# Encoder layer with experts: x tiles turned inside spans of 256 tokens, the first expert's row list by one-hot products, the last output tile in another order, the value slices asked for sooner

## The reference, cut to what matters

```python
def encoder(x, ...):                                  # x_prompt: 256 tokens, x_sample: 1024 tokens, D = 1024
    xn = rmsnorm(x, norm1_g)
    proj = xn @ w_in                                  # columns: pool u (512), q, k, v, o (512 each), 16 gates
    a = multiscale_pool(proj[u], pool_w, pool_scale)
    m = bidir_mlstm(proj, gate_b, head_norm_g)        # 4 heads of 128, chunks of 128 tokens, two directions
    x = x + concat(a, m) @ w_out
    xn2 = rmsnorm(x, norm2_g)
    x = x + hier_moe(xn2, ...)                        # best of 4 groups, best 2 of its 8 experts, SwiGLU
    return rmsnorm(x, final_norm_g)

def hier_moe(xn, ...):
    # each token chooses 2 of 32 experts; rows are sorted by expert, in blocks of 128
    hb = silu(xb @ w_gate[e]) * (xb @ w_up[e])        # 1024 x 512 each
    y  = hb @ w_down[e]                               # 512 x 1024
    return segment_sum(y[dest] * weight, token)
```

## Time and profile before

| what | us |
|---|---|
| median of 3 runs | 1238.58 (1236.71 to 1238.65) |
| the profiled execution, its own time | 1236.62 |
| its span, first to last instruction | 1234.9 |
| TensorE matmul busy | 1113.7 (90%) |
| VectorE busy | 866.8 (70%) |
| ScalarE busy | 684.6 (55%) |
| mean granted TensorE clock | 0.962 |

### The profile page before, as it was taken

The page is one execution under the profiler, slowest core; times in us unless marked ns, Lnnn a source line. Parts: engine busy times, 40 slices in busy tenths (PEclk is TensorE's granted clock), DMA queues, the critical chain, the costliest instruction groups (busy, mean ns, idle before and its releaser), DMA issues.

```text
span 1234.9 us, 17854 instructions
## 1 busy us (share of the span) xinstructions
PE 1113.7 (90%) x5679; PEld 935.0 (76%) x5679; DVE 866.8 (70%) x1340; ACT 684.6 (55%) x1128; POOL 185.3 (15%) x285
## 2 busy tenths in 40 slices
PE   5999999998998999992899999999999999999910
PEld 4888888887888788881688888888888888888710
DVE  5649510234447656665688999999999999999958
ACT  5432241233346544213677877877787787787623
POOL 1100210011100012223011211221221221121100
PEclk9999999999999899995899999999999999999965
DMA  8212240455979344446789999999999999999667
GB/s 236 59 29 83 86 129 1 142 175 199 318 265 334 130 139 151 163 154 228 269 313 374 372 377 385 378 380 391 382 380 394 382 378 391 383 372 387 241 251 298
DMA packets 135808, 324.04 MB, mean 262 GB/s; under 512 B 23552, under 2 KB 60320, under 8 KB 135760
## 3 DMA queue, kind: packets, MB, share of 16 engines
q1 hardware_dynamic: 119856, 281.80, 63.1%
q0 software_dynamic: 15904, 41.61, 8.7%
HBM read 285.35 MB, written 51.11 MB: 272 GB/s over the span
## 4 chain that ended last, share of the span: by engine, by line
PE 78%; DVE 9%; ACT 6%; DMA 3%; issue 3%; POOL 0%; ACTq 0%; SPq 0%; POOLq 0%; DVEq 0%
PE psum L808 23%; PE psum L810 22%; PE psum L809 22%; DVE e_lo L1723 3%; ACT e_hi L1284 3%; PE psum L1024 2%; PE psum L979 1%; PE psum L1057 1%; ACT h_fb L1241 1%; DVE x L1834 1%; DVE x L1842 1%; PE psum L922 1%; DVE x L1832 1%; PE psum L863 1%; PE psum L967 1%
## 5 line engine op out<-in xcount | busy, mean ns | idle before, releaser
L1723 DVE TENSOR_TENSOR e_lo<-e_st,e_hi 128x1024 fp32r<-128x1024 f32 x384 | 442.6, 1219 | 15.6 <-ACT e_hi L1284 14.4
L1284 ACT ACTIVATE e_hi<-e_st 128x1024 fp32r<-128x1024 f32 x384 | 372.3, 1053 | 9.4 <-PE psum L810 8.4
L808 PE MATMUL psum<-e_hi,ex_hi 128*128 128x512 f32 x512 | 203.8, 398 | 8.6 <-DVE ex_lo L1765 3.7
L810 PE MATMUL psum<-e_hi,ex_lo 128*128 128x512 f32 x512 | 200.8, 392 | 0.0
L809 PE MATMUL psum<-e_lo,ex_hi 128*128 128x512 f32 x512 | 200.3, 391 | 0.0
L808 PE MATMUL psum<-xT_hi,w_hi 128*128 128x512 f32 (+1 forms) x408 | 147.1, 361 | 4.5 <-DVE xT_lo L1403 3.0
L809 PE MATMUL psum<-xT_lo,w_hi 128*128 128x512 f32 (+1 forms) x408 | 145.4, 356 | 0.0
L810 PE MATMUL psum<-xT_hi,w_lo 128*128 128x512 f32 (+1 forms) x408 | 145.3, 356 | 0.0
L808 PEld LDWEIGHTS psum<-e_hi,ex_hi 128*128 128x128 f32 x512 | 96.6, 189 | 41.4 <-DVE e_lo L1723 16.3
L810 PEld LDWEIGHTS psum<-e_hi,ex_lo 128*128 128x128 f32 x512 | 96.5, 189 | 20.8
L809 PEld LDWEIGHTS psum<-e_lo,ex_hi 128*128 128x128 f32 x512 | 96.6, 189 | 19.3
(11 more groups left out here) (234 smaller groups left out, 1722.3 us busy)
## 6 DMA issues: line engine op xcount, KB each, us to landing
e_st<-in_expert_w_gate_dram SPq DMA_DIRECT2D x128, 512.0 KB, 4.7
e_st<-in_expert_w_up_dram SPq DMA_DIRECT2D x128, 512.0 KB, 7.3
e_st<-in_expert_w_down_dram SPq DMA_DIRECT2D x128, 512.0 KB, 8.6
mlstm_units<-stage SPq DMA_DIRECT2D x18, 640.0 KB, 3.8
w_st<-in_w_in_dram SPq DMA_DIRECT2D x20, 512.0 KB, 4.1
xn_scratch<-xn POOLq DMA_DIRECT2D x20, 512.0 KB
f_y<-expert_rows SPq DMA_DIRECT2D x20, 512.0 KB, 12.1
stage<-gate_rows SPq DMA_DIRECT2D x18, 512.0 KB, 6.0
```

The costliest lines, as they stand in the source:

```text
L808: pe.matmul(out, a_hi, b_hi, start=start, stop=False)
L810: return pe.matmul(out, a_lo, b_hi, start=False, stop=stop)
L1284: act.activation(e_hi[:, r, :, :], e_st[:, slot, :, :], ACT.Copy).then_inc(ehi_done, 1)
L1723: dve.tensor_tensor(e_lo[:, r, :, :], e_st[:, slot, :, :], e_hi[:, r, :, :].bitcast(F32), ALU.subtract).then_inc(elo_done, 1)
```

## The change

1. Start. The first six products are the three pool slices over tokens 0 to 255 and then over 256 to 511 (`SPANS`), in place of three over 0 to 511. Only tiles 0 and 1 are turned before them; tiles 2 and 3 inside products 0 and 1, the others behind products 2 to 6. Small products on the identity (`keep_warm`) stand between. ScalarE and VectorE run roots, norms and splits in a written order (`x_root`, `x_norm`). Slices 1 and 2 and x tile 2 are asked for when tile 1 has landed; the gate slice comes before the other constants; the gate bias has a semaphore of its own.
2. SyncE asks for slices 19 and 20 at block 6 of its loop, ahead of that block's store.
3. Output stage. The heads of tile 2 are turned after tile 0's products and its squares are taken later. For the last tile, ranks and turns of the tiles before it are put between halves of its products, the turned last tile is copied before its squares are taken, and filler products (`keep_busy`, 128 x 512 into a free bank) stand around the router.
4. First list. `list_rows` also compares the slot number of expert 0 with a ramp, which gives a one-hot matrix of token by slot for each tile. Ten products with `token_parts` (token in tile, tile, second choice, one) give, per slot, the row number; three VectorE operations make `first_row` of it, and the first gather uses it. The last list entries are written after that gather is issued; the other lists go the old way.
5. `gx` is set to zero when the turn of the output loop on GpSimd reaches tile 8. The last router's weights are worked out later. Four pieces of expert 1 are asked for when the first gather has landed, ahead of the load of the lists.
6. Expert rows are turned and split in two halves with a signal each, in all steps.

```diff
-        proj += [("u", U + c, 0) for c in range(NG - 1)]
+        proj += [("u", U + c, NS + half) for half in range(2) for c in range(NG - 1)]
...
             slice_in(0)
+            sp.wait_ge(x_load[1], 16)
             slice_in(1)
+            slice_in(2)
+            sp.wait_ge(bias_zero, 1)
...
+            slice_in(G)
...
-                if i == N_EARLY - 1:
+                if i == N_EARLY - 2:
                     for m in (NSL - 2, NSL - 1):
                         slice_in(m)
                 block_out(i)
...
+            sp.wait_ge(gx_load[0], 16)
+            for c in range(4):
+                gu_in(1, c)
             for i in range(2):
                 sp.wait_ge(list_out[i], 16 * NT)
...
             for i, t in enumerate(order):
+                if i == NT - 2:
+                    pool.wait_ge(hT_ready, NT)
+                    pool.memset(gx[:, :, :], 0.0).then_inc(gx_zero, 1)
+                if i == NT - 1:
+                    entries_out(i - 1)
                 pool.wait_ge(xn2_done, i + 1)
...
             pool.wait_ge(gx_zero, 1)
+            pool.wait_ge(totals_read, 1)
+            rows_in(0, 0)
+            entries_out(NT - 1)
             pool.wait_ge(first_rows, 16)
-            rows_in(0, 0)
             rows_in(1, 1)
...
+            keep_warm(8)
+            x_transposes(0)
+            keep_warm(3)
+            x_transposes(1)
+            keep_warm(8)
+            transposed_inside = {0: 2, 1: 3}
+            transposed_after = {2: (4,), 3: (5,), 4: (6,), 5: (7,), 6: (8, 9)}
...
+            out_rows(NT - 1, 0, 0, 4)
+            ranks(NT - 3)
+            x1_transposes(NT - 2)
+            out_rows(NT - 1, 0, 4, KD)
+            router(NT - 2)
+            out_rows(NT - 1, 1)
+            keep_busy(4)
+            x1_transposes(NT - 1)
+            ranks(NT - 2)
+            keep_busy(3)
+            router(NT - 1)
+            keep_busy(18)
             ranks(NT - 1)
-            pe.wait_ge(slots_done, NT)
+            pe.wait_ge(slots_done, 2 * NT - 1)
             for t in range(NT):
-                last = pe.matmul(psum[:, 7, 128:128 + E], onesb[:, :], chosen[:, t, :], start=(t == 0), stop=(t == NT - 1))
-            last.then_inc(count_ready, 1)
+                last = pe.matmul(psum[:, 7, 200:204], one_hot_rows[:, t, :], token_parts[:, t, :], start=(t == 0),
+                                 stop=(t == NT - 1))
+            last.then_inc(totals_ready, 1)
...
+            keep_busy(20)
...
+                dve.tensor_copy(token_parts[:, t, 2:3], both[:, E:E + 1])
+                dve.scalar_tensor_tensor(out=one_hot_rows[:, t, :], in0=slot_ramp[:, :], scalar=rank[:, 0:1],
+                                         in1=chosen[:, t, 0:1].broadcast_to([P, P]), op0=ALU.is_equal,
+                                         op1=ALU.mult).then_inc(slots_done, 1)
...
+            dve.wait_ge(totals_ready, 1)
+            link(dve.tensor_tensor(rt[:, 324:328], psum[:, 7, 200:204], part_sizes[:, :], ALU.mult))
+            link(dve.tensor_reduce(rt[:, 328:329], rt[:, 324:328], AX.X, ALU.add))
+            dve.tensor_scalar(first_row[:, :], rt[:, 328:329], 2.0 * T, None, ALU.add).then_inc(totals_read, 1)
```

More of the change, by code:

```diff
@@ L491, in _ @@
                 sp.dma_start(dst, src).then_inc(consts_in, 16)
[L492 to L498, removed]
+            for m in range(G + 1, NSL - 2):
                 slice_in(m)
@@ L647, in _, with step @@
                          blocks[:, 1:NT, :]).then_inc(later_rows, 16)
-            def step(i):
-                for c in range(8):
+            def step(i, first=0):
+                for c in range(first, 8):
                     gu_in(i, c)
@@ L652, in step @@
                     down_in(down_piece(i, c), i - 1, c)
-            step(1)
+            step(1, first=4)
             step(2)
@@ L690, in _ @@
                                pattern=[[-1, P]], channel_multiplier=1).then_inc(consts_done, 1)
-            for t in range(3, NT):
+            pool.wait_ge(x_load[1], 16)
+            for t in range(2, NT):
                 x_in_tile(t)
@@ L992, in _, with keep_busy @@
             pe.wait_ge(consts_done, N_CONST)
-            for t in range(NT + 1):
+            def keep_busy(count):
+                for n in range(count):
+                    pe.matmul(psum[:, 4, :], mix_hi[1][:, n % KD, :], mix_hi[1][:, 0:4, :], start=True, stop=True)
+            for t in range(NT - 1):
                 if t == 0:
@@ L1017, in _ @@
-            last.then_inc(count_ready, 1)
+                last = pe.matmul(psum[:, 7, 200:204], one_hot_rows[:, t, :], token_parts[:, t, :], start=(t == 0),
+                                 stop=(t == NT - 1))
+            last.then_inc(totals_ready, 1)
+            for t in range(NT):
+                last = pe.matmul(psum[:, 5, 0:E], onesb[:, :], chosen[:, t, :], start=(t == 0), stop=(t == NT - 1))
+            last.then_inc(totals_ready, 1)
+            keep_busy(20)
             def ex_transposes(i, b):
@@ L1021, in ex_transposes @@
                 pe.wait_ge(gx_load[b], slot_loads(i, b))
-                wait(pe, exlo_done, i)
-                for k in range(KD):
-                    last = pe.transpose(psum[:, 2 + k // 4, (k % 4) * P:(k % 4 + 1) * P], gx[:, b, k:D:KD], ident[:, :])
-                last.then_inc(ext_ready, 1)
+                wait(pe, exlo_done, 2 * i)
+                for half in range(2):
+                    for k in range(4 * half, 4 * half + 4):
+                        last = pe.transpose(psum[:, 2 + half, (k % 4) * P:(k % 4 + 1) * P], gx[:, b, k:D:KD], ident[:, :])
+                    last.then_inc(ext_ready, 1)
@@ L1173, in _, with x_root @@
             act.wait_ge(root_done, 1)
-            for t in range(NT):
+            def x_root(t):
                 if t == 0:
@@ L1298, in _ @@
                     act.wait_ge(xn2_done, NT)
-                    for c in range(6):
+                    for c in range(4):
                         hi_part(gu_piece(0, c))
@@ L1349, in step @@
                 ht_hi_part(i, b)
+            for c in range(4, 6):
+                hi_part(gu_piece(0, c))
             ex_hi_part(0, 0)
@@ L1414, in _, with x_norm @@
             dve.wait_ge(g1_in, 16)
-            for t in range(NT):
+            def x_norm(t):
                 dve.wait_ge(root_done, t + 2)
@@ L1798, in step @@
                 ht_lo_part(i, b)
-            for c in range(2):
+            for c in range(4):
                 lo_part(gu_piece(0, c))
             dve.memset(rows_to[:, NT * E:NT * E + 1], 2 * T).then_inc(no_row, 1)
-            for c in range(2, 6):
+            ex_lo_part(0, 0)
+            for c in range(4, 8):
                 if c == 5:
```

180 lines of the change are left out of this document (115 added, 65 removed).

## The result

| | median us | runs | ratio to before, 95% interval |
|---|---|---|---|
| before | 1238.62 | 4 | |
| changed | 1219.97 (1217.44 to 1222.09) | 4 | 0.9849 [0.9825, 0.9873] |
| changed, run again beside the later experiments | 1219.60 (1216.72 to 1220.45) | 5 | 0.9843 [0.9821, 0.9866] |

The change makes the kernel 18.65 us faster; 23.5 were forecast. The first profiled execution of the changed kernel took 1222.09 us (span 1220.3, clock 0.968), the slowest of its four. The rows are from the first, unless the text says otherwise. One of the nine executions of the kernel before that stand beside the last four experiments was slow (2320.14 us) and isn't in the ratios.

What follows compares the result with a forecast made beforehand. TensorE was taken as the bound in expert loop and output stage, with three gaps to cut. Start 6, value slices 4.5 and passage 13 sum to 23.5 us off 1236.6, plus 2.0 for the median: 1215, range 1208 to 1224.

Steps and rivals of the forecast that it cites:

- the passage: From output stage to experts: shorter chain to the first gather and first expert products, 13 us won, bounds 9 to 16.5.
- the start: First products begin at 15.5 instead of 22.55, clock kept up by small products: 6 us won, bounds 2 to 8.4.
- the signs that the prediction names for being wrong: Early waits for xn or w_lo, gather waiting for normed-row stores, clock 0.50 after the last tile, loop step over 18.3 us.
- the start wins nothing: Rival: ScalarE or a late tile paces the first six products; start worth 0 to 1 us, total 1220.5; chance 0.13.
- Value slices: Near 284 us: slices 19 and 20 asked for one block sooner, 4.5 us won, bounds 0 to 5.
- (a): Last tile's expert choice: moved memset wins 2.1 us, router at full clock 0.4; done at 566.6 instead of 569.05.
- (b): From last choice to first gather's issue: one-hot way takes 2.5 us instead of 7.85; issue at 569.1.
- (c): First gather's flight: 5.0 us instead of 8.7, as nothing is queued; landed at 574.1 instead of 585.6.
- (e): Expert 0's gate and up: 10.9 us at full clock instead of 12.9; expert 1's rows wanted 16.2 us sooner.
- (d): From first gather's landing to first expert product: 1.8 us instead of 4.5, by halves and at full clock.
- (f): Expert 1's rows late: list load queued behind four weight loads, gather takes 8.2 us, TensorE waits 3.2 us.
- The list held long: Rival: list behind eight weight loads, gather of 10.3 us, low clock; passage worth 6, total 1222; chance 0.09.

Runs made afterwards that it cites:

- the second trace: Second profiled execution of the unaltered changed kernel, from the timing beside the later experiments, the fastest of its five: 1216.72 us (span 1215.0, clock 0.973).
- 5.7 us for three: Changed kernel with expert 0's second 2 MB behind the stores, list loads ahead of expert 1's weights, and zeroing behind the next-to-last tile's stores: 1213.86 us, ratio 0.9795.
- 8.6 for all five: Changed kernel with those three edits, VectorE's remainders held until the first gather is issued, and 28 filler products instead of 20: 1211.03 us, ratio 0.9786.
- VectorE's hold alone: Changed kernel with only VectorE's four remainders of expert 0's weights made to wait until GpSimd has issued the first gather: 1218.69 us, ratio 0.9841.

## Why the prediction was right, and where it was off

**Direction and range: right, with some luck.** 1219.97 lies in 1208 to 1224 and in the likeliest case's own range, at its upper end. But the passage brought less than its stated lower bound of 9 us by every way of counting but one (5.3 by the medians; from the last residual on 6.0 and 8.3 up to expert 1's turn, 5.8 and 9.2 up to the end), and the start more than its upper bound of 8.4 by the medians (8.8). The 2.8 us too little at the start made up for part of the 7.7 too much at the passage. Of the signs that the prediction names for being wrong, two came: the gather waited for the stores, and the clock fell behind the last tile in spite of the filler (0.77 between 550 and 555 us, 0.50 between 570 and 573). The first expert product comes 16.6 us sooner, not 24.7.

**Start, forecast 6: a little too low.** 8.8 us alone on the kernel before by the medians, 7.7 by the marks at 158 us, and 6.3 at the last residual of the start's own trace, behind its fall of the clock. The first product comes at 14.72, 0.8 sooner than the sum had it, and its successors at once at 0.12 us apart, so the 2.2 us of the clock came in full. Of the 2.7 us that TensorE waits for `xn`, 1.29 and 1.15 lie before the first product and 0.27 behind it (0.3 forecast). So what stands against the gain came to 7.8 + 2.2 - 7.7 = 2.3 us by the marks, not 3.4: turning tiles inside the products and the narrow spans cost 1.1 less than priced, or something else up to 158 us gained it; no run separates the two. The rival "the start wins nothing" is out. Not foreseen was the fall of the clock at 160 us, which took back 2.4 + 1.0 = 3.4 us in the profiled execution (5 us at 0.52, 5 us at 0.80). The kernel before lost nothing there (1.00).

**Value slices, forecast 4.5: right.** 4.6 us alone; 5.0 by the marks (9.3 - 7.7 + 3.4), wait behind qT 0.7.

**Passage, forecast 13: too high; about 5.3 by the medians, 6.0 and 8.3 in the two traces up to expert 1's turn.** By the steps:

(a) From the last residual to the last choice 10.78 us (557.57 - 546.79) against 13.43: 2.65 won, for 2.45 forecast. In this execution the filler around the router ran at the low clock and took 5.99 us, 0.9 past the choice; in the second trace it took 4.36 and was hidden. The moved zeroing met the choice of tile 7, as foreseen, but held VectorE for 2.3 us instead of 1.8, and TensorE lost 1.3 us to it instead of 0.9. Moving it behind the next stores is worth 4.1 us by the medians, of which 1.3 are explained.

(b) **This is the step that failed**: "Issue at 569.1", with 2.5 us from the choice to the gather. The path of small operations took 3.0 us (2.2 in the second trace), but from the choice to the issue it was 7.1 (557.57 to 564.65): the gather had to wait for the stores of the normed rows, which the prediction names among the things that would make it wrong, and didn't price. The sum followed the list's path alone, since that was the long one before; with it cut to 2 or 3 us, two others set the issue. One is the stores, 9.1 us long, at least 5.2 of them because 2 MB of weights are asked for just ahead. The other is VectorE's 4.6 us of remainders, which the prediction has nowhere: they let the issue end 0.93 us behind them, the same moment. With both lifted, the gather is issued 13.9 us after the last residual (558.94 - 545.06), where the sum has 13.5: then the term is right, and what is left is the gather's own flight of 7.47 us. From the last residual to the landing 18.5 us were forecast and 23.0 measured (22.1 in the second trace): 4.5 us.

(c) Landing in 5.0: 5.16, which is luck. The reason given, that nothing is queued by then, fits the late issue (DMA share 0.00 between 565 and 567 us). Issued as early as the sum has it, and beside weights, the gather took 7.47 and 6.62 us, in the two kernels with both holds lifted. (e) Gate and up 10.9: 10.9. (d) 1.8 us from the landing to the first product: 3.6, since the clock was at 0.50 when the rows came (turn 1.97 us instead of 1.05, five fillers 2.2 us). With filler up to the landing it is 2.2.

(f) The mechanism was right and was shown by undoing it; TensorE waited 3.6 us for 3.2 forecast. The list took 1.7 us longer than the sum had it (9.6 us from the first landing to the second gather's issue, for 7.9) and the gather 8.75 for 8.2. So 18.4 us from the first landing to expert 1's turn, for 15.9: 2.5 us. 4.5 + 2.5 are the 7.0 us between 13 and 6.0. Undone, the list costs TensorE no wait.

**The other rivals.** Expert 1's rows weren't in time. The loop isn't slower, so the signals by halves cost nothing that shows. The list held long comes nearest in its time (1222), but its mechanism (eight weight loads ahead and a gather of 10.3 us) was not it. In the range, each term low by half its distance gives 1215 + 6.25 = 1221.3 and not 1222; nothing hangs on it.

**Left open.** Why the clock falls near 160 us in every kernel with the new start (0.50 to 0.67 between 160 and 165 us in all twelve traces) and not in the two traces with the old start, which run the same transposes of 36 columns 8 us later at 1.00. How much of the gather's longer flight is the weights beside it. And 2.8 of the 4.1 us that the zeroing's place is worth.

## What to carry to other kernels

When a long chain is cut, list every other condition of the instruction at its end, with the time at which each is met now, before pricing the cut: here two others (stores, VectorE's run) ended within 1 us of each other, the gather's flight grew when both were out of the way, and lifting either one alone gave nothing. What an engine wins ahead of a wait that another chain sets is given back at that wait, so edits in one passage are worth trying together (5.7 us for three, 8.6 for all five, by the medians) and from the last wait backwards. A small load that others wait for belongs ahead of the large ones on its queue: 4.9 us less from its issue to the gather that needs it, for a few moved lines.

## What the runs showed of the hardware

- The issue of an indirect gather on GpSimd took 5.17 us in three kernels, while VectorE ran four operations of two inputs (128 x 1024, 4.61 us in a row), and ended 0.9 us after them; with VectorE held it took 1.05 us (three kernels). The issue waited for the end of all four operations, not of one (1.21 us). By the Trainium skill (SBUF — State Buffer, section SBUF: two separate sides) VectorE and GpSimd share a pair of ports that one of them holds for a whole instruction; it says that GpSimd can't write a DMA's descriptors while VectorE runs in a two-port mode, and that an operation of VectorE with two inputs blocks only a GpSimd operation that reads SBUF. The durations agree if the gather's issue counts as such a read, which that section doesn't say.
- The stores of one normed tile (2 x 512 KB) took 9.1 us from the second one's issue behind 2 MB of loads (8.9 to 9.3 in the traces of five other kernels or timings), and at most 3.9 us without.
- A zeroing of 1.84 us on GpSimd held an operation of VectorE on four columns for 2.57 us instead of 0.23. The trace has the operation begin 0.7 us before the zeroing (528.88 and 529.58) and end with it.
- A run of TensorE on matmuls alone doesn't keep the clock in every case: it was busy for 5.00 of 5.00 us between 155 and 160 on products of 256 and 36 columns, and in the next 5 us the granted clock was 0.52.
- A granted clock just under 1.00 need not cost time. In the profiled execution with VectorE's hold alone the column reads 0.95 nearly throughout, also from 620 to 1130 us, where TensorE is busy for 505.50 of 510 us; the second trace of the changed kernel reads 1.00 there and has 505.45.
